# VectorE's order in the heads: four pieces of work get other places

## The reference

```python
def gated_delta_chunked(q, k, v, beta, g):
    gam = jnp.cumsum(g, axis=-1)
    Lmat = jnp.exp(jnp.where(incl, gam[..., :, None] - gam[..., None, :], -jnp.inf))
    kb = k * beta[..., None]
    A = jnp.where(strict, jnp.einsum('bhntk,bhnsk->bhnts', kb, k) * Lmat, 0.0)
    T = lax.linalg.triangular_solve(eye + A, eye, left_side=True, lower=True, unit_diagonal=True)
    u, w = T @ (v * beta), T @ (kb * exp(gam))
    qk = jnp.einsum('bhntk,bhnsk->bhnts', q, k) * Lmat
...

def hgrn2_chunked(q, k, v, log_f):
    b_cum = jnp.cumsum(log_f, axis=3)
...
```

## Time and profile before

| | |
|---|---|
| median of 3 runs | 1387.07 us (1386.98 to 1387.5) |
| the profiled execution | 1387.15 us |
| its span | 1385.4 us |
| TensorE's granted clock over the span | 0.999 |
| PE, DVE, ACT busy | 1367.5, 1026.2, 803.8 us |
| period of a head, from one identity copy to the next | 50.93 to 50.95 us |

### The profile page before, as it was taken

One profiled execution on the slowest core, in us unless ns is written; L12 is line 12 of the kernel. 1 busy time (PEld: TensorE's weight loads), 2 busy tenths in 40 slices (PEclk: granted clock), 3 DMA queues, 4 the chain that ended last, 5 costly groups with the idle time before them and its releaser, 6 DMA issues.

```text
span 1385.4 us, 25241 instructions
## 1 busy us (share of the span) xinstructions
PE 1367.5 (99%) x9092; PEld 1237.7 (89%) x9092; DVE 1026.2 (74%) x1601; ACT 803.8 (58%) x1310; POOL 23.4 (2%) x71
## 2 busy tenths in 40 slices
PE   8999999999999999999999999999999999999998
PEld 8999999988888888888899999999999898888887
DVE  5786787677666686666788888888888877666665
ACT  4445554644344354444678898898898844544443
POOL 6000000000000000000000000000000000000000
PEclk9999999999999999999999999999999999999999
DMA  8565555556555746566564445535444276566661
GB/s 266 149 191 147 146 147 159 186 184 209 183 182 192 232 133 203 182 182 194 152 172 131 134 115 138 142 99 156 132 104 145 89 186 213 154 204 196 199 189 61
DMA packets 298383, 227.82 MB, mean 164 GB/s; under 512 B 10882, under 2 KB 280404, under 8 KB 298324
## 3 DMA queue, kind: packets, MB, share of 16 engines
q1 hardware_dynamic: 298324, 227.01, 55.2%
HBM read 225.90 MB, written 1.08 MB: 164 GB/s over the span
## 4 chain that ended last, share of the span: by engine, by line
PE 92%; DVE 3%; ACT 3%; DVEq 1%; issue 1%; ACTq 0%; POOL 0%; POOLq 0%
PE G L1971 8%; PE G L1973 8%; PE G L1972 8%; PE M L1988 7%; PE G L1988 7%; PE M L1976 7%; PE M L1977 7%; PE M L1978 6%; PE G L1990 4%; PE M L1990 4%; PE G L2711 2%; PE G L2091 2%; PE G L1976 2%; PE G L1978 2%; PE G L1977 2%; PE M L2537 1%
## 5 line engine op out<-in xcount | busy, mean ns | idle before, releaser
L1156 DVE TENSOR_TENSOR w_lo<-w_raw,w_hi 128x2048 fp32r<-128x2048 f32 (+2 forms) x249 | 480.5, 1936 | 156.4 <-ACT w_hi L624 153.3
L624 ACT ACTIVATE w_hi<-w_raw 128x2048 fp32r<-128x2048 f32 x198 | 377.8, 1909 | 174.1 <-PE G L1973 74.8
L1971 PE MATMUL G<-xa,w_hi 128*128 128x256 f32 x992 | 292.2, 295 | 0.0
L1973 PE MATMUL G<-xa,w_lo 128*128 128x256 f32 x992 | 280.2, 282 | 0.0
L1972 PE MATMUL G<-xa,w_hi 128*128 128x256 f32 x992 | 280.1, 282 | 0.0
L1971 PEld LDWEIGHTS G<-xa,w_hi 128*128 128x128 f32 x992 | 189.4, 191 | 1.9 <-DVE w_lo L1156 0.7
L1972 PEld LDWEIGHTS G<-xa,w_hi 128*128 128x128 f32 x992 | 189.6, 191 | 0.0
L1973 PEld LDWEIGHTS G<-xa,w_lo 128*128 128x128 f32 x992 | 189.2, 191 | 0.0
L1976 PE MATMUL M<-w_hi,xb 128*128 128x512 f32 x304 | 119.0, 391 | 0.6 <-DVE xb L1156 0.5
L1977 PE MATMUL M<-w_lo,xb 128*128 128x512 f32 x304 | 118.7, 390 | 0.0
L1978 PE MATMUL M<-w_hi,xb 128*128 128x512 f32 x304 | 118.3, 389 | 0.0
(11 more groups left out here) (405 smaller groups left out, 2515.4 us busy)
## 6 DMA issues: line engine op xcount, KB each, us to landing
w_raw<-in_w_in SPq DMA_DIRECT2D x150, 512.0 KB, 4.9
w_raw<-in_ffn_w_in SPq DMA_DIRECT2D x88, 512.0 KB, 5.0
w_raw<-in_w_ff SPq DMA_DIRECT2D x64, 512.0 KB, 4.2
w_raw<-in_ffn_w_out SPq DMA_DIRECT2D x44, 512.0 KB, 4.8
w_raw<-in_w_in SPq DMA_DIRECT2D x33, 256.0 KB, 3.2
w_raw<-in_w_out SPq DMA_DIRECT2D x16, 512.0 KB, 4.2
w_raw<-in_w_branch_gdn SPq DMA_DIRECT2D x16, 512.0 KB, 5.2
w_raw<-in_w_branch SPq DMA_DIRECT2D x12, 512.0 KB, 4.2
```

Of the source, the lines that this page charges most:

```text
L624: nc.scalar.activation(w_hi[:, slot, :], w_raw[:, slot, :], ACT.Copy).then_inc(hi_ready, 1)
L1156: return v.tensor_tensor(dst, src, hi.bitcast(F32), ALU.subtract)
L1971: mm(out_, w[0], x[0], start=first, stop=False)
L1973: return mm(out_, w[1], x[0], start=False, stop=last_)
```

## The change

VectorE's order alone changes; nothing is added or removed but one drain. In every `head`: `inverse(6)` goes before `tap(2, 2)`; the identity copy goes from behind the exponents to a place in front of `w_low_j(2)`; the second half of the low part goes from the head's end to a place in front of the triangle; the scans and the keys go from there to behind `y0_ready`, with a `settle()` of their own.

```diff
             scored(7)
+            inverse(6)
             tap(2, 2)
-            inverse(6)
...
             if main and gemm:
                 hgrn_gate(i)
+            if gemm:
+                v.tensor_copy(yi, ident[:].unsqueeze(1).unsqueeze(1).to_broadcast([P, TT, 2, P]))
             w_low_j(2)
...
-                v.tensor_copy(yi, ident[:].unsqueeze(1).unsqueeze(1).to_broadcast([P, TT, 2, P]))
                 w_low_half(c0 + 3 + RING, 0, i, 6)
                 dve.wait_ge(lt_ready, i + 1)
                 diag = lt.rearrange("p e (b c) -> p e b c", b=3)[:, :, 0:3:2, :]
                 v.tensor_tensor(diag, diag, tri[:].unsqueeze(1).unsqueeze(1).to_broadcast([P, 2, 2, P]), ALU.mult)
-                dve.wait_ge(lnf_ready, i + 1)
-                for b in range(TT):
-                    v.tensor_tensor_scan(hb[:, P * b:P * b + P], ones[:], hf[:, P * b:P * b + P], 0.0, ALU.mult, ALU.add)
-                v.scalar_tensor_tensor(out=hk, in0=eh, scalar=lb1[:, ds(i, 1)], in1=hr,
-                                       op0=ALU.mult, op1=ALU.mult).then_inc(qk_ready, 1)
+                w_low_half(c0 + 3 + RING, 1, i, 6)
                 settle()
                 dve.wait_ge(kq_done, i + 1)
...
                 v.drain().then_inc(y0_ready, 1)
+                dve.wait_ge(lnf_ready, i + 1)
+                for b in range(TT):
+                    v.tensor_tensor_scan(hb[:, P * b:P * b + P], ones[:], hf[:, P * b:P * b + P], 0.0, ALU.mult, ALU.add)
+                v.scalar_tensor_tensor(out=hk, in0=eh, scalar=lb1[:, ds(i, 1)], in1=hr,
+                                       op0=ALU.mult, op1=ALU.mult).then_inc(qk_ready, 1)
+                settle()
                 if main:
                     delta_out_low(i)
...
                 v.tensor_copy(tok[:, 0, :], G[:, 1, :]).then_inc(evac[1], 1)
-                w_low_half(c0 + 3 + RING, 1, i, 6)
             settle()
```

## The result

The changed kernel takes 1390.26 us (median of 12 runs, 1389.89 to 1390.88) against 1387.07 us (12 runs, 1386.8 to 1387.5): a ratio of 1.0023, with an interval of 1.0015 to 1.0031. Every run of the changed kernel lies above every run of the other. The profiled execution took 1390.08 us, 2.93 more than that of the kernel before, its span 1388.4 us. In the code after the change the lines up to 1859 keep their numbers; the exponents are L1882, the mask L1890, `nt` L1897, its copy into `yi` L1900, the scans L1904, the keys L1905, `mt` L1912, the scaled `lt` L1915, `inv_z` L2539, the piece behind `inverse(6)` L2609 and the transposes of `yi` L2689.

The account below looks back on a forecast made before the run. A path through ScalarE and VectorE's tail, returning at `lt2_ready`, was taken to bind TensorE: 0.48 - 0.06 = 0.42 us in each of 7 tails, 2.9 us on 1387.15, 1390.05 (1390.0 in median terms); range 1387.0 to 1391.6.

Parts of the forecast that it names:

- `lt2_ready` decides, not the loop's turn: At L2537, a new head's first piece: TensorE's load waits for VectorE's `lt2_ready` from L1912, with only 0.12 us between.
- faster: Rival, chance 0.13: L2537 waits for the turn of TensorE's loop, so both removed stalls are gain, 2.8 us: 1384.3.
- The chain that ended last says the same: At the last full head's end the chain runs along VectorE, with L1912 in it, and only then back to TensorE.
- The identity copy is free: In VectorE's tail: its 0.34 us cost nothing in the new place, in front of an idle 1.19 us.
- `y0_ready` comes 0.75 us sooner: In VectorE's tail: L1903 ends at 877.09 instead of 877.84, more than the 0.46 us L2687's loads stand idle.
- The two pauses, 0.14 and 0.33: In VectorE's tail: 0.14 us behind the drain signalling `y0_ready`, 0.33 behind the new `settle()` in front of L1643.
- Small pauses: Rival, chance 0.27: both new pauses near 0.09 us, L1912 0.19 later, TensorE loses 0.13 a head: 1388.0.
- L1643 is 0.48 us later: In VectorE's tail: L1643 starts at 878.67 against 878.19, with bounds 0.19 to 0.71, and delays `lt2_ready` as much.
- 0.06 us of slack behind L1912: Between L1912's end and L2537's load: the 0.12 us there may hold 0.06 of slack, subtracted from the 0.48.
- What TensorE gains at L2607 and L2687 it spends waiting at L2537: On TensorE: gains of 0.14 to 0.24 us at L2607 and 0.16 at L2687 become waiting at L2537.
- Nothing is lost there: At L2537 in the kernel before: it starts 0.23 us behind its neighbour, so its idle load costs TensorE nothing.
- Head 0 loses nothing: In head 0: L1912 ends about 1.2 us later, near 728.2, and its load wants 728.26, so nothing is lost.

Follow-up runs that it names:

- the later output: The kernel before, with only the output's low part moved behind the two differences: 1386.36 us, ratio 0.9994.
- the half alone: The kernel before, with only the second half of the low part moved in front of the scans: 1391.12 us, ratio 1.0028.
- the two last kernels: Reordered changed kernel with a quarter low part before the logarithm's wait: 1386.09 us; the same with the first difference between `y0_ready`'s drain and the keys: 1385.47 us.
- a quarter early: Against the changed kernel: quarter instead of half low part, scans before the triangle, no drain behind the keys, second difference behind the scaled `lt`'s drain: 1386.09 us.
- the drain later: The changed kernel, with the new drain moved from behind the keys to behind the output's low part: 1388.40 us, ratio 1.0010.

## Why the prediction was right

The time (1390.0 forecast, 1390.26 measured), the period (51.4 and 51.36), the place and the sign are as forecast. The sign is clear of noise; the size, 3.19 us, is just above the 2.8 us that the prediction took as the least that can be told. That the loss of 0.42 us a head comes out to the hundredth is luck: L1915 came 0.02 less late than taken, 0.06 of slack was not there, and 0.04 came back at another place. The steps, one by one:

- *`lt2_ready` decides, not the loop's turn.* Right. The row of TensorE names L1915 (the list of loads still says "issue"), and the later output took the idle time away while the loop turned as before. With that the rival "faster" falls. `evac[1]`, which came as much later, adds nothing: from the first piece to the first multiplication of the projection it is 0.67 us in both kernels (881.19 to 881.86, 882.51 to 883.18).
- *"The chain that ended last says the same."* It does not. Between the two rows it runs on along VectorE, through L1916 (1084.82) and L1743 (1087.64), and comes back to TensorE at 1088.43, 4 us after L1912, at a later step of the inverse in head 8. The witnesses for `lt2_ready` are the row of TensorE and the later output.
- *The identity copy is free.* Right: its own run shows no change. VectorE's idle time in front of the low part fell from 1.19 to 0.87 us, by the copy's 0.32.
- *`y0_ready` comes 0.75 us sooner.* Right: 0.76, and no load waits for it.
- *The two pauses, 0.14 and 0.33.* Right: 0.11 (877.95 to 878.06) and 0.32 (879.18 to 879.50). "Small pauses" had 0.09 for both. The Trainium skill, "VectorE: DVE Perf Modes", section "The DRAIN you can't avoid", has a flush behind every VectorE instruction, whether a semaphore follows or not. The prediction read from it that the new drain would be free; the section speaks of that flush and not of a drain that the program writes out. Moving the written drain takes 0.21 us out of each head, so the measurement decides against that reading.
- *L1643 is 0.48 us later.* Measured 0.45.
- *0.06 us of slack behind L1912.* Wrong in its reason, and small. From the end of the scaled `lt` to the load it is 0.12 us in both kernels, so there was no slack. Instead 0.04 came back: before, the load of L2486 waited for the second half of the low part (882.66 to 882.83, where its neighbours are 0.12 apart), which now ends long before. By starts it is 2.22 us from L2537 to L2518, the piece behind L2486 (881.19 to 883.41), and 2.18 after (882.51 to 884.69). 0.46 - 0.04 is 0.42 us, by which the period grew.
- *"What TensorE gains at L2607 and L2687 it spends waiting at L2537."* Right in the sum, wrong in the place for L2607. With `inverse(6)` alone first, L2537 waits no longer; TensorE runs into ScalarE's L1083 and into `y0_ready`. The changed kernel has the same wait for L1083, 1.9 us. TensorE was thus bound at two signals of one path, `y0_ready` and `lt2_ready`, with L1083 not far from it, and a delay shows at whichever comes first: at L2687 with the half alone, at L2539 with the scans behind.
- *"Nothing is lost there"* at L2537 before. Wrong: the start was on time, but the four multiplications took 0.70 us, 0.62 without the wait, and 0.08 us a head was to be had there.
- *Head 0 loses nothing.* Right: its L1915 ends at 728.18 and its load comes at 728.30 without idle time.

Of the loss the second half is the part that can be undone alone: without it the changed kernel stands at 1387.04. The scans behind `y0_ready` cost 0.09 us a head by themselves. With the drain at another place 1388.40 is left. These three accounts overlap and don't add, since the half and the scans both draw on the same wait of the triangle for TensorE (0.53 us with the scans gone from there, 0.75 with the identity copy gone too).

## What to carry to other kernels

When the busiest engine is full and others return signals to it just in time, shortening the way to one signal by moving work behind it lengthens the way to the next: count each move at all the signals that leave the engine behind it, and the change is worth the worst of them. Work at the end of a loop's turn, where an engine waits anyway, moves in front of a signal for free only into a wait of its own length; here a wait of 0.75 us took in that much of a piece of 1.22 and left 0.47 a head, while a quarter, cut to the size of the wait for the logarithm, went into it whole. Directly behind a drain belongs an instruction whose addresses don't come from a loop's counter, as the two last kernels show (0.23 us of pause against none).

## What the runs showed of the hardware

The pause behind a drain depends on the instruction behind it. The chain of work that ended last, in the changed kernel around the two drains (start, duration, piece; "DVEq" is VectorE's sequencer):

```profile
877.95 0.03 DVEq L1901
877.98 0.09 issue
878.06 0.12 DVE arena L1904
...
878.81 0.38 DVE arena L1905
879.18 0.10 issue
879.28 0.10 DVEq L1643
879.38 0.04 issue
879.42 0.04 DVEq L1643
879.46 0.04 issue
879.50 0.75 DVE xb L1643
```

In front of the scans there are 0.11 us, in front of L1643 0.32, and in these the sequencer runs two instructions of L1643's own line. L1643 reads one operand and writes another at places that depend on the loop's counter; the scans, L1699 and the triangle have fixed places and paused 0.09 to 0.12 behind a drain in these traces, though the scans and the triangle wait for a semaphore's value that the counter sets. The keys read one operand, a scalar for each partition, at a place that depends on the counter, and here one trace holds both cases. In the kernel "a quarter early" they stand behind the drain of `y0_ready`; in head 0, which is written out ahead of the loop with a constant for the counter, and in head 1, the loop's first:

```profile
723.73 0.74 DVE L1911 COPY_PREDICATED arena<-masks,arena 128x512 f32<-128x512 int32 x1
724.59 0.48 DVE L1913 SCALAR_TENSOR_TENSOR arena<-arena 128x256 f32<-128x256 f32 x1
...
774.65 0.76 DVE L1911 COPY_PREDICATED arena<-masks,arena 128x512 f32<-128x512 int32 x1
775.64 0.48 DVE L1913 SCALAR_TENSOR_TENSOR arena<-arena 128x256 f32<-128x256 f32 x1 [0.23 <-issue]
```

The view of the keys' line counts their instruction eight times, and one of the sequencer only in the seven heads of the loop:

```profile
L1913 DVEq FUSED_REGOPS  x7: 71/71/71, 775.5 to 1080.3; - x7
```

From the copy's end to the keys it is 0.12 us with the constant and 0.23 with the counter. So the address costs the keys 0.11 us. L1643, with two such operands, pauses some 0.2 longer than instructions with fixed places; that its addresses cost this is concluded from the keys and from its two instructions of the sequencer, since behind a drain it stands nowhere with a constant. Behind undrained work neither paused at all: with the drain later, the sequencer runs the first of L1643's two at 877.61, while VectorE is still at the scans. The Trainium skill, "Perfetto Trace Analysis", section "Per-engine timelines", has a drain done by the sequencer itself, which reads the next instruction only behind it. By that the preparation of an address is bare behind a drain and can run beside work where there is none. The traces agree: 0.23 and 0.32 us behind a drain, no pause without one.

A load that stands idle "until issue" can be waiting for a semaphore: the 0.24 us at L2537 went away when the signal came 0.21 us sooner, though the list of waits and the order of time of the kernel before did not name it.
